# A hybrid retention and state-space block on one core: side work moved between weight chunks, and the last half column computed in two parts

## The reference, cut to what matters

```python
def reference(x, ...):
    h = rmsnorm(x, norm_mix_g)
    proj = h @ w_in                                   # 256 x 2048 @ 2048 x 5120
    q = rope(proj[..., 0:R]);  k = rope(proj[..., R:2 * R])
    v, g, u = proj[..., 2 * R:3 * R], proj[..., 3 * R:4 * R], proj[..., 4 * R:]
    y_ret = retention_group(q, k, v, g, ret_gn_g)     # 8 heads of 128
    y_ssm = s5_group(u, ...)                          # 64 groups of 16 channels, 64 complex states each
    x = x + concatenate([y_ret, y_ssm]) @ w_out
    h = rmsnorm(x, norm_ffn_g)
    x = x + (silu(h @ w_gate) * (h @ w_up)) @ w_down  # hidden width 5632
    return rmsnorm(x, norm_final_g)
```

## Time and profile before

| what | value |
|---|---|
| median of three executions | 1135.8 us (1135.53 to 1135.96) |
| the profiled execution's own time | 1136.07 us |
| its span (first to last instruction) | 1134.2 us |
| PE busy | 1118.7 us (99%) |
| DVE busy | 714.5 us (63%) |
| ACT busy | 532.3 us (47%) |
| POOL busy | 87.5 us (8%) |
| mean HBM and SBUF traffic by DMA | 198 GB/s |

### The profile page before, as it was taken

How to read it: one execution, slowest core, us unless ns; L and a number is a source line. 1 busy time by engine, 2 the same in 40 slices (tenths; PEclk the granted TensorE clock), 3 DMA queues, 4 the chain that set the end, 5 groups by cost and what they waited for, 6 DMA issues and landing times.

```text
span 1134.2 us, 15132 instructions
## 1 busy us (share of the span) xinstructions
PE 1118.7 (99%) x5608; PEld 925.3 (82%) x5608; DVE 714.5 (63%) x781; ACT 532.3 (47%) x637; POOL 87.5 (8%) x130
## 2 busy tenths in 40 slices
PE   9999999999999999999999999999999999999996
PEld 6888777888988888888888888888888888888885
DVE  7999997556765655464555646455564645556466
ACT  7669444345744553434344343434434343443443
POOL 7120233320100000000000000000000000000000
PEclk9999999999999999999999999999999999999998
DMA  9883787854755567566665666666565666656552
GB/s 363 281 235 114 204 244 229 253 174 130 255 198 193 170 209 216 185 190 190 195 188 185 200 185 188 191 195 188 186 200 185 188 190 195 187 186 201 186 186 93
DMA packets 115095, 224.81 MB, mean 198 GB/s; under 512 B 8432, under 2 KB 13808, under 8 KB 114416
## 3 DMA queue, kind: packets, MB, share of 16 engines
q1 hardware_dynamic: 110832, 214.18, 60.6%
q0 software_dynamic: 3808, 9.31, 3.3%
q10 hardware_dynamic: 416, 0.79, 0.2%
HBM read 218.09 MB, written 5.11 MB: 197 GB/s over the span
## 4 chain that ended last, share of the span: by engine, by line
PE 84%; DVE 10%; DMA 3%; issue 1%; ACT 1%; POOL 0%; SPq 0%; POOLq 0%; DVEq 0%; ACTq 0%
PE ps L1374 26%; PE ps L1375 26%; PE ps L1376 26%; DVE w_lo L767 3%; DMA raw<-in_w_in 3%; PE ps L1596 1%; PE ps L1668 1%; PE ps L1669 1%; PE ps L1670 1%; DVE wb L894 0%; DVE wb L892 0%; PE ps L1496 0%; ACT w_hi L432 0%; DVE cl_t L967 0%; DVE wb_t L893 0%
## 5 line engine op out<-in xcount | busy, mean ns | idle before, releaser
L767 DVE TENSOR_TENSOR w_lo<-raw,w_hi 128x1024 fp32r<-128x1024 f32 x384 | 468.2, 1225 | 384.9 <-ACT w_hi L432 384.5
L432 ACT ACTIVATE w_hi<-raw 128x1024 fp32r<-128x1024 f32 x384 | 407.3, 1061 | 569.4 <-PE ps L1376 518.7
L1374 PE MATMUL ps<-w_hi,actA_hi 128*128 128x512 f32 x576 | 227.0, 394 | 2.4 <-DVE w_lo L767 2.4
L1375 PE MATMUL ps<-w_lo,actA_hi 128*128 128x512 f32 x576 | 224.3, 389 | 0.0
L1376 PE MATMUL ps<-w_hi,actA_lo 128*128 128x512 f32 x576 | 224.3, 389 | 0.0
L1376 PE MATMUL ps<-w_hi,h2B_lo 128*128 128x512 f32 x352 | 137.0, 389 | 0.0
L1374 PE MATMUL ps<-w_hi,h2B_hi 128*128 128x512 f32 x352 | 136.9, 389 | 0.0
L1375 PE MATMUL ps<-w_lo,h2B_hi 128*128 128x512 f32 x352 | 136.9, 389 | 0.0
L1374 PEld LDWEIGHTS ps<-w_hi,actA_hi 128*128 128x128 f32 x576 | 108.1, 188 | 26.4 <-issue 2.6
L1376 PEld LDWEIGHTS ps<-w_hi,actA_lo 128*128 128x128 f32 x576 | 108.1, 188 | 22.8
L1375 PEld LDWEIGHTS ps<-w_lo,actA_hi 128*128 128x128 f32 x576 | 108.2, 188 | 21.5
(11 more groups left out here) (250 smaller groups left out, 976.3 us busy)
## 6 DMA issues: line engine op xcount, KB each, us to landing
raw<-in_w_gate SPq DMA_DIRECT2D x88, 512.0 KB, 3.7
raw<-in_w_up SPq DMA_DIRECT2D x88, 512.0 KB, 3.7
raw<-in_w_down SPq DMA_DIRECT2D x88, 512.0 KB, 3.6
raw<-in_w_in SPq DMA_DIRECT2D x79, 512.0 KB, 5.4
raw<-in_w_out SPq DMA_DIRECT2D x32, 512.0 KB, 3.8
k_tab<-k_scratch POOLq DMA_DIRECT2D x64, 64.0 KB, 3.8
raw<-in_ssm_w_glu SPq DMA_DIRECT2D x8, 512.0 KB, 3.6
x_tok<-in_x_tok SPq DMA_DIRECT2D x2, 1024.0 KB, 7.9
```

The lines of the kernel that those rows point to most:

```text
L432: nc.scalar.activation(w_hi[:, s % SPL], raw[:, s % RAW], ACT.Copy).then_inc(S["high_done"], 1)
L767: tt(w_lo[:, s % SPL], raw[:, s % RAW], w_hi[:, s % SPL].bitcast(F32), ALU.subtract).then_inc(S["low_done"], 1)
L1374: mm(o, x_hi, h, start=first, stop=False)
L1375: mm(o, x_hi, l, start=False, stop=False)
```

## The change

Five numbers or groups of numbers in the tables of side work move, and the last part of the second token half is cut in two.

- `BACK_AT`: `turn_back(1)` from chunk 45 to 43.
- `CL_AT`: `cl_table(3)` from 42 to 45.
- `K_AT`: `k_tables(3)` from 44 to 46. `Y_AT`: `y_batch(3)` from 53 to 55.
- `QK_AT`: `rotate(0)` from 43 to 48 and `rotate(1)` from 51 to 53 (59 and 67 stay). `QK_TR`: `qk_transposes(0)` from 45 to 50, `qk_transposes(1)` from 53 to 55.
- The end: the part (column 3, t = 1) becomes two parts of 256 columns with twelve matmuls each; every one of the five parts now has a PSUM bank of its own. DVE scales two pieces of 640 columns of the second token half, ACT 768 columns. POOL adds the first half's sum as before, and folds the second one's into one scaled addition (a second L1364-like operation) ahead of the reciprocal root.

```diff
-BACK_AT = (35, 45)
-CL_AT = (30, 36, 38, 42, 47, 50, 55, 60)
-K_AT = (33, 38, 40, 44, 49, 52, 57, 62)
-Y_AT = (43, 47, 49, 53, 57, 65, 67, 71)
+BACK_AT = (35, 43)
+CL_AT = (30, 36, 38, 45, 47, 50, 55, 60)
+K_AT = (33, 38, 40, 46, 49, 52, 57, 62)
+Y_AT = (43, 47, 49, 55, 57, 65, 67, 71)
...
-QK_AT = tuple(GRP * (gi + 1) + 3 for gi in (4, 5, 6, 7))
-QK_TR = (45, 53, 65, 69)
+QK_AT = (48, 53, 59, 67)
+QK_TR = (50, 55, 65, 69)
...
-LAST_ORDER = ((0, 0), (0, 1), (1, 0), (1, 1), (2, 0), (3, 0), (2, 1), (3, 1))
-LAST_BANK = {2: 6, 3: 0}
-OUT_PARTS = ((0, slice(0, 1024)), (0, slice(1024, 2048)),
-             (1, slice(0, 512)), (1, slice(512, 1024)), (1, slice(1024, 1536)))
+LAST_ORDER = tuple((t, slice(NCOL * c, NCOL * (c + 1))) for c, t in ((0, 0), (0, 1), (1, 0), (1, 1), (2, 0), (3, 0), (2, 1))
+                   ) + ((1, slice(1536, 1792)), (1, slice(1792, 2048)))
+LAST_BANK = (6, 0, 7, 1, 2)
+OUT_PARTS = ((0, slice(0, 1024)), (0, slice(1024, 2048)), (1, slice(0, 640)), (1, slice(640, 1280)))
+ACT_PART = slice(1280, 2048)
...
                 pool.wait_ge(S["fin_sq"], 6 + 2 * t)
-                link(tt(ss[:, R_FIN, one], ss4[:, 1, 0, one], ss4[:, 1, 3, one], ALU.add))
-                link(ts(ss[:, R_FIN, one], ss[:, R_FIN, one], 1 / D_MODEL, EPS, ALU.mult, ALU.add))
-                rsqrt(rstd[:, R_FIN, one], ss[:, R_FIN, one], S["rstd_fin_ready"], 1)
+                link(tt(mean, ss4[:, 1, 0, one], ss4[:, 1, 3, one], ALU.add))
+                link(ts(mean, mean, 1 / D_MODEL, EPS, ALU.mult, ALU.add))
+                if t:
+
+                    pool.wait_ge(S["fin_sq"], 9)
+                    link(ts(mean, ss4[:, 0, 0, one], 1 / D_MODEL, mean, ALU.mult, ALU.add))
+                rsqrt(rstd[:, R_FIN, one], mean, S["rstd_fin_ready"], 1)
```

More of the change, by code:

```diff
@@ L127 @@
 SQUARES_AT = 8
-LAST_ORDER = ((0, 0), (0, 1), (1, 0), (1, 1), (2, 0), (3, 0), (2, 1), (3, 1))
-LAST_BANK = {2: 6, 3: 0}
-OUT_PARTS = ((0, slice(0, 1024)), (0, slice(1024, 2048)),
-             (1, slice(0, 512)), (1, slice(512, 1024)), (1, slice(1024, 1536)))
+LAST_ORDER = tuple((t, slice(NCOL * c, NCOL * (c + 1))) for c, t in ((0, 0), (0, 1), (1, 0), (1, 1), (2, 0), (3, 0), (2, 1))
+                   ) + ((1, slice(1536, 1792)), (1, slice(1792, 2048)))
+LAST_SUM = ((1, 0), (1, 0), (1, 1), (1, 1), (1, 2), (1, 3), (1, 2), (1, 3), (0, 0))
+LAST_BANK = (6, 0, 7, 1, 2)
+OUT_PARTS = ((0, slice(0, 1024)), (0, slice(1024, 2048)), (1, slice(0, 640)), (1, slice(640, 1280)))
+ACT_PART = slice(1280, 2048)
 def build(nc, A, out):
@@ L730, in _ @@
                 high(TAIL0 + c)
-            for i, (c, t) in enumerate(LAST_ORDER):
+            for i, (t, at) in enumerate(LAST_ORDER):
                 act.wait_ge(S["last_added"], i + 1)
@@ L734, in _ @@
                     act.wait_ge(S["fin_sq"], i)
[L735 to L738, removed]
+                kind, slot = LAST_SUM[i]
+                nc.scalar.activation(y1T[:, 0:2].rearrange("p a s -> p (a s)")[:, 0:at.stop - at.start],
+                                     x2[:, t, at], ACT.Square,
+                                     accum_out=ss4[:, kind, slot, t:t + 1]).then_inc(S["fin_sq"], 1)
+            act.wait_ge(S["gain_done"], 7)
             act.wait_ge(S["rstd_fin_ready"], 2)
-            at = slice(NCOL * 3, NCOL * 4)
+            at = ACT_PART
             nc.scalar.activation(x_gain[:, 1, at], x_gain[:, 1, at], ACT.Copy, scale=rstd[:, R_FIN, 1:2]
@@ L1214, in finish_part @@
             def finish_part(i):
-                col, t = LAST_ORDER[i]
-                at = slice(NCOL * col, NCOL * (col + 1))
+                t, at = LAST_ORDER[i]
                 dve.wait_ge(S["last_mm"], i - 3)
@@ L1220, in finish_part @@
                     dve.wait_ge(S["cols_added"], 4 * FG + 4)
-                tt(x2[:, t, at], ps[:, LAST_BANK[col] + t], x2[:, t, at], ALU.add).then_inc(S["last_added"], 1)
+                tt(x2[:, t, at], ps[:, LAST_BANK[i - 4], 0:at.stop - at.start], x2[:, t, at], ALU.add
+                   ).then_inc(S["last_added"], 1)
                 dve.wait_ge(S["last_added"], i + 1)
@@ L1225, in scale_parts @@
             def scale_parts(which):
-                dve.wait_ge(S["gain_done"], 4 + 2 * which)
+                dve.wait_ge(S["gain_done"], 4 + 3 * which)
                 dve.wait_ge(S["rstd_fin_ready"], which + 1)
@@ L1247, in _ @@
             finish_part(7)
+            finish_part(8)
             scale_parts(1)
@@ L1359, in _ @@
                 one = slice(t, t + 1)
+                mean = ss[:, R_FIN, one]
                 pool.wait_ge(S["fin_sq"], 5 + 2 * t)
@@ L1734, in _ @@
                 column_chunk(None, i % SPL, ff_pair(ffE_hi, ffE_lo, 2 * k), 6 - 2 * (col % 2), k == 0, k == 1)
-            for i, (col, t) in enumerate(LAST_ORDER[4:]):
+            for i, (t, cols) in enumerate(LAST_ORDER[4:]):
                 tok = slice(P * t, P * (t + 1))
+                col, start = divmod(cols.start, NCOL)
+                width = cols.stop - cols.start
                 if i == 0:
@@ L1744, in _ @@
                         ready(n)
-                    at = slice(NCOL * (k % 2), NCOL * (k % 2 + 1))
-                    ins = three(ps[:, LAST_BANK[col] + t], ffE_hi[:, k, tok], ffE_lo[:, k, tok],
+                    at = slice(NCOL * (k % 2) + start, NCOL * (k % 2) + start + width)
+                    ins = three(ps[:, LAST_BANK[i], 0:width], ffE_hi[:, k, tok], ffE_lo[:, k, tok],
                                 w_hi[:, n % SPL, at], w_lo[:, n % SPL, at], k == 0, k == 3)
```

## The result

The changed kernel takes 1142.33 us (median of 4 executions, 1142.09 to 1143.30) against 1135.88 us before in the same comparison: ratio 1.0055, 95% interval 1.0043 to 1.0067. It is slower by 6.45 us by the medians, 6.2 by the ratio. The forecast was slower, 1140.3 us, range 1139.2 to 1142.6: the sign and the range hold, but the likeliest case was 2 us short, and the rival "the clock falls in the pause" (1142.2 us) is what happened. Of the two signs that the prediction named for its forecast being wrong, one did not come (PE's longest wait is 4.4 us and not under 3) and one did: the matmuls behind that wait show a lower clock. The profiled execution took 1142.09 us, its span 1140.3.

A forecast was written before the change was run, and what follows sets the result against it. The prediction took PE to be the pace, with waits for DVE's low parts. Its terms, -1.81 + 1.6 + 4.6 + 0.1 = +4.5 us, put the profiled execution at 1140.6 and the forecast at 1140.3 us, range 1139.2 to 1142.6.

The forecast's parts named there:

- the clock falls in the pause: Rival: PE's clock drops in the pause before chunk 56, adding 1.9 us, 1142.2 us in all; chance 0.27.
- two signs: Forecast wrong if PE's longest wait is under 3 us, or if the matmuls behind it show a lower clock.
- What bounds the kernel: Whole kernel: PE sets the pace, waiting 3.9 us for DVE's low parts; other engines' waits are slack.
- Part 1: Chunks 42 to 50: waits before 43 and 44 go, -1.81 us; about 1.6 us come back later.
- give-back of 1.6: Chunks 46 and 49: DVE's work comes later, so new PE waits return about 1.6 of the 1.81 us.
- the wait before 46: Before chunk 46: PE waits 0.5 us for DVE's low part, about 0.6 with the pause's extra.
- The wait before 49: Before chunk 49: PE waits 0.9 us for DVE's low part, 1.0 with the pause's extra.
- Part 2: Chunks 54 to 56: table 6 must wait for batch 3, so PE stands still 4.6 us before chunk 56.
- The moves that I costed at nothing: Part 2's other moves: `qk_transposes(0)` behind 50, `k_tables(3)` behind 46, batch 3's kernel finished behind 50; no cost.
- Part 3: The end: the last 512 columns in two halves and new output pieces cost +0.1 us, bounds -0.5 and +0.9.
- A rule against the change: Mid-kernel pause of 4.6 us: the skill page says long idle gaps halve PE's clock; loss 1.4 to 2.7 us.
- The sum: Whole kernel: -1.81 + 1.6 + 4.6 + 0.1 = +4.5 us, forecast 1140.3 us.

The follow-up runs named there:

- one-chunk variant: Kernel before with batch 3 and the second q/k transposes issued with chunk 54 instead of 53: 1138.23 us, ratio 1.0020.
- the one move alone: Kernel before with only batch 3 and the second q/k transposes moved from behind chunk 53 to behind 55: 1142.68 us, ratio 1.0061.
- The kernel with the wait of 2.09 us: Kernel before with other side-work tables, among them second scan behind chunk 42, second turn back behind 46, table 6 behind 57: 1136.26 us, ratio 0.9996.

## Why the prediction was right or wrong

- **What bounds the kernel.** Right: PE's starts are the clock of everything, and nothing of what ACT, DVE or POOL waited for came into the sum.
- **Part 1, -1.81 and +1.6.** Right in mechanism, with the give-back of 1.6 somewhat too large in most executions. Alone it gives -0.16 in the trace; in the changed kernel's profiled execution -0.77, and -0.50 to -0.67 in the four other traces with these tables. What differs is the wait before 46, and it follows the swap, which landed in 7.36 us where I had taken 7.78. Runs show 7.36 to 7.94, and the wait grows with it (nothing at 7.36, 0.08 us at 7.58, 0.46 at 7.94). The wait before 49 was sized at 0.9 and measured 0.57 to 0.62.
- **Part 2, +4.6.** Right: the traces with the clock held up give +4.63 and +4.64, the wait itself is 4.44, and it stands before chunk 56 as forecast. The moves that I costed at nothing cost nothing (with the table moved to 57, chunks 53 to 77 take the 86.68 us of before). The one-chunk variant (+1.97, from 4.6 - 2.72 = 1.9) shows that the arithmetic behind the term carries over.
- **Part 3, +0.1.** Right: +0.13 in the changed kernel, +0.14 alone.
- **"A rule against the change", and the chance of its rival.** This is the step that failed, and the stated range was wide enough to hold the outcome all the same. I had the mechanism and its price, 1.9 us (measured 1.68 in one execution, 2.81 in another), but gave it 0.27 and let the sum go by a clock that stays up. My argument against it was that the pause is "only just" of the length after which the earlier trace rows show the fall, and that transposes stand directly ahead of it. The fall was there in both profiled executions of the changed kernel and in that of the one move alone, and of the eight executions of the changed kernel the six without a trace had mean granted clocks of 0.994 or 0.995. The earlier trace rows gave too kind a bound, since a single place of one execution shows one pause length that the clock survived, not the longest it always survives: here it fell in one execution behind 2.09 us. The Trainium skill's page "TensorE: Matmul & The Clock Gate" (section "HAM oscillation — how this bites in real kernels") describes matmuls that start at half clock behind a wait for data. The trace agrees in kind. In size the stretches give (1 - 0.62) x 2 / 0.5 + (1 - 0.53) x 2 / 0.5 = 3.4 us at the lower level in one execution and in the same way 6.8 in the other, of which PE was waiting through the first 1. Half of the time at the lower level in which PE had matmuls to run is 1.7 and 2.9 us, within 0.1 us of the measured 1.68 and 2.81: the lower clock accounts for what came on top of the pause.
- **The sum.** -0.77 + 4.63 + 1.68 + 0.13 = +5.7 by the trace against +4.5: the term left out is the clock's, and part 1 came out 0.6 better in that execution. The medians differ by 6.45, more than the profiled execution shows; its mean clock is 0.996 and that of the other three 0.994, as in the second trace with the longer fall. That they had the longer fall too fits, but is not shown, for they have no trace.

## What to carry to other kernels

When a step on a busy engine overwrites a buffer of another engine's step, moving the reader later moves the writer too, and everything written behind it; look for the slot's earlier user before a step is put later, and keep enough of the other engine's work between the two (here the table and the low part take 5.2 us, two chunks of PE's). Cost a pause of TensorE at its length, and from what these runs show a fall of the clock on top of one of 4.4 us, and possibly of one of 2.1. When low parts no longer hold PE up, the next wait here is a buffer on its way through HBM, whose landing has to be reckoned with in the tables too.

## What the runs showed of the hardware that I had not expected

- A pause of 4.44 us in which PE did nothing costs 1.7 to 2.8 us on top of its length. In one execution the first slow matmul is the fourth after the pause, 0.77 us after PE had begun again; in another it is the first.
- In the two kernels whose traced waits are 2.09 us (11 executions) and 2.35 us (4) the clock fell in some executions and not in others of the same program: a trace shows the fall behind 2.09 and another none behind 2.35, the rest is read from the mean clocks and times. Behind 1.99 us (11 executions) and 1.69 us (10), all at a mean clock of 0.997 or 0.998, there is no sign of it. The kernel with the wait of 2.09 us has two groups of times, about 1.7 us apart by their medians (1134.8 and 1136.5), which looks like noise if the clocks aren't read beside them.
- Idle matmuls (18 of them, shown as 36 records, 4.18 us) in the pause kept the clock up in the one trace of them and cost nothing, since PE would have waited anyway. It is a repair only where the pause can't be removed; removing it gave about 6 us by the medians, filling it 1 to 2.
